# Matmul operands laid out anew: normed tiles 1280 bytes apart, weight blocks at one place modulo 256, small vectors moved into the gaps

## The chip, the cores and the metric

The kernel runs on one core of a Trainium2 chip. The metric is device time in microseconds of one execution; several runs are made and their median is compared. A profiled execution gives a trace of every instruction.

## The reference

Two transformer blocks run one after the other on 256 tokens of width 1024, in fp32. The first has a mixer of mLSTM heads and latent attention, a cross attention to 256 memory tokens, and a feed-forward layer of width 4096. The second prepends 16 meta tokens (272 columns from there on), has a SwiGLU layer of width 2816, a mixer of windowed attention and gated linear attention, and a second SwiGLU layer. Nearly all the work is products of a normed activation with a weight matrix:

```python
h = rmsnorm(x, norm_ffn_g[l])
x = x + jnp.square(jax.nn.relu(h @ w_ff1[l])) @ w_ff2[l]
...
h = h + 0.5 * swiglu(rmsnorm_2(h, ffn1_norm[l]), ffn1_w_gate[l], ffn1_w_up[l], ffn1_w_down[l])
u = rmsnorm_2(h, mix_norm[l])
(aq, ak, av, gq, gk, gv, gr, g_low, gate_a, gate_b) = jnp.split(u @ w_in[l], offsets, axis=-1)
```

## The kernel before

**Products.** Activations lie transposed in SBUF: a tile holds 128 of the 1024 features on the partitions and all tokens along the row. A product `h @ w` is made of 128x128 weight blocks (stationary, loaded by LDWEIGHTS) with 256 or 272 moving columns, in fp32r. To keep fp32 accuracy both sides are split into a high and a low part, so each block costs three matmuls, called a triple here: `wh` with the high tile (L1046), `wh` with the low tile (L1047), `wl` with the high tile (L1048). The pairs of tiles are `U`/`UL` (normed input, 8 tiles), `H`/`HLO` (hidden layer, up to 22 tiles) and `Y`/`YL` (heads' outputs). There are 2304 triples.

**Weights.** SP loads a unit of up to 1024 columns (two 128-row blocks of 512 columns, as a rule) into one of six `raw` buffers. ScalarE copies it to `wh` (L1385), VectorE subtracts to get `wl` (L1819). `wh` and `wl` have four halves each, `PITCH` elements apart; the low part of a unit lies in the other half of its pair (`low_half`). A unit serves four output tiles, so a unit of two blocks is eight triples. Then the next unit follows.

**Order.** A planner (`Plan`) writes one list of steps; PE, ScalarE and VectorE each run their part of it in that order. The second mixer is woven from many chains by a table of letters.

**Places in SBUF.** While TensorE streams one tile, it already loads the weights of the next matmul. Which places of SBUF these two reads touch at one time is set by three things:

- where tile k of `U` starts: with 256 columns the tiles are packed 1024 bytes apart (`part`). With 272 columns they are 1088 bytes apart, so their starts step by 64 bytes modulo 256;
- where a weight block starts in its half: `first_columns` shifts the blocks of the products named in `skew` by 16 elements (64 bytes) a step, until the block's place modulo 256 fits the number of its tile k;
- `wh` begins 64 bytes past the start of `U`, modulo 256 (the assertion on 320 modulo 1024 in `build`).

```python
skew = {"sw1": 0, "dn1": 0, "in2": g == 2, "gvr": g, "gab": 1}.get(name)
...
while skew is not None and (n * width // 16 + shift - k - skew) % 4:
    shift += 1
```

So the block for tile k lies 64 bytes past tile k modulo 256. That holds between the two matmuls of a pair as long as both belong to tiles of equal k modulo 4. `same_place` orders the blocks as k, k+4 for this reason: inside a unit the distance stays at 64. Where one unit ends and the next begins, the stream is tile k+4 and the weights loaded under it belong to tile k+1, so the distance is 128 there. The first group of `sw1` and the first groups of `in2` and `gvr` (`plain=1`) take k in plain order 0, 1, 2, ... and have other distances at nearly every block.

`sw1` and `dn1` are the first SwiGLU layer (272 columns), `in2`, `gvr` and `gab` the input products of the second mixer (272 columns, or 256 starting 64 bytes into the tile for the names in `NO_META`). `ff1a`, `ff1b`, `ff2a`, `ff2b` are the feed-forward layer of the first block, `sw2` and `dn2` the second SwiGLU layer; these have 256 columns.

**Small vectors.** Nine tiles of 6 to 32 elements a row (`gcol`, `emc`, `HST`, `DC`, `ST`, `ST2`, `nsink`, `QRS`, `QKG`) hold gate columns, softmax sums and the like. They lie between `vec` and `X`; `beyond` then pads so that `X` starts at 64 modulo 256.

Of the kernel before, what the change touches and what calls it, by code (L numbers as in the profile page):

```python
# [8 lines left out]
F32 = mybir.dt.float32  # L9
F32R = mybir.dt.float32r  # L10
# [4 lines left out]
P = 128  # L15
# [3 lines left out]
T2 = 272  # L19
# [1 line left out]
FF1 = 4096  # L21
FF2 = 2816
SLOT = 1024
PITCH = 1152
NRAW = 6
NHL = 4
SL = 4 * T2
# [225 lines left out]
def first_columns(name, g, i):  # L253


    ks, width = GEMM[name].units(g)[i], GEMM[name].width(g)
    skew = {"sw1": 0, "dn1": 0, "in2": g == 2, "gvr": g, "gab": 1}.get(name)
    at, shift = [], 0
    for n, k in enumerate(ks):
        while skew is not None and (n * width // 16 + shift - k - skew) % 4:  # L260
            shift += 1
        at.append(n * width + 16 * shift)
    return at
# [7 lines left out]
def split_blocks(parts, half, name, g, i):  # L271
    at, width = first_columns(name, g, i), GEMM[name].width(g)
    step = at[1] - at[0] if len(at) > 1 else width
    assert all(a == at[0] + n * step for n, a in enumerate(at)) and at[0] + len(at) * step <= PITCH
    return parts[:, half, at[0]:at[0] + len(at) * step].rearrange("p (k c) -> p k c", c=step)[:, :, 0:width]
# [618 lines left out]

def part(t, name, k, n):

    at = SL * (k // 4) + n * (k % 4) if name in ("Y", "YL") else n * k
    return t[name].rearrange("p k c -> p (k c)")[:, at:at + n]


def streamed(t, name, k, tag):

    if name in ("small", "uv", "o", "wq_x", "ff1a", "ff1b", "sw2"):
        return part(t, "U", k, T1), part(t, "UL", k, T1)
    if name in ("sw1", "in2", "gvr", "gab"):
        a = NMETA if name != "sw1" and tag[0] in NO_META else 0
        return t["U"][:, k, a:T2], t["UL"][:, k, a:T2]
    if name in ("memk", "memv", "ff2a", "ff2b", "out2", "dn2"):
        return part(t, "H", k, T1), part(t, "HLO", k, T1)
    if name == "dn1":  # L910
        return t["H"][:, k, :], t["HLO"][:, k, :]
    if name in ("uq", "ukv"):
        k = 2 if name == "ukv" else k
        return t["CQH"][:, k, :], t["CQL"][:, k, :]
    return part(t, "Y", k, T1), part(t, "YL", k, T1)
# [1512 lines left out]
def pool_program(e, t, plan, ev):  # L2428

    at, up = ev.at, ev.up  # L2430
    e.memset(t["GT"][:, :, :], 0.0).then_inc(*up("filled", "gates"))
    e.wait_ge(*at("filled", "gates"))
    e.memset(t["SY3"][64:128, 0:256], 0.0).then_inc(*up("filled", "squares"))
    e.wait_ge(*at("filled", "squares"))
    e.memset(t["S"][64:128, SL + 512:SL + 768], 0.0).then_inc(*up("filled", "key"))
    e.wait_ge(*at("filled", "key"))
    e.memset(t["QB"][0:64, :], 0.0).then_inc(*up("filled", "mlstm"))
    e.wait_ge(*at("filled", "mlstm"))
    e.wait_ge(*at("angle", 0))
    e.memset(t["S"][0:64, SL + 768:SL + 1024], 0.0).then_inc(*up("filled", "second_key"))  # L2440
    e.wait_ge(*at("gates", "max"))
    e.dma_start(t["d_max"], t["GT"][0:4, 3, :]).then_inc(*up("out_max", 0, by=16))
    e.wait_ge(*at("out_max", 0))
    e.dma_start(t["S"][:, 8 * SL:8 * SL + 1024].rearrange("p (h c) -> p h c", h=4),
                t["d_max"].partition_broadcast(128)).then_inc(*up("in_max", 0, by=16))
# [68 lines left out]
def build(nc, aps, out):  # L2514
    with ExitStack() as ctx:
        def sb(name, shape, dt=F32):
            return ctx.enter_context(nc.sbuf_tensor(name, shape, dt))

        def beyond(residue, modulus, name):
            if (residue - nc.sbuf_base) % modulus:  # L2520
                sb(name, [P, (residue - nc.sbuf_base) % modulus // 4])

        t = dict(aps)
        t["out"] = out
        t["cst"] = sb("cst", [P, NLAST])
        t["vec"] = sb("vec", [P, NVEC])
        t["gcol"] = sb("gcol", [P, 16])
        t["emc"] = sb("emc", [P, 8])
        t["HST"] = sb("HST", [P, 4, 8])
        t["DC"] = sb("DC", [P, 8])  # L2530
        t["ST"] = sb("ST", [P, 2, 6])
        t["ST2"] = sb("ST2", [P, 2, 16])
        t["nsink"] = sb("nsink", [P, 8])
        t["QRS"] = sb("QRS", [P, 8])
        t["QKG"] = sb("QKG", [P, 8])
        beyond(64, 256, "before_x")
        t["X"] = sb("X", [P, 8, T2])
        base = nc.sbuf_base
        for n in ("U", "UL"):
            t[n] = sb(n, [P, 8, T2], F32R)  # L2540

        for i, n in enumerate(("Y", "YL")):
            at = nc.sbuf_base
            t[n] = sb(n, [P, 8, T2], F32R)
            assert nc.sbuf_base == at + 8 * T2 * 4
            for j in range(2):
                t[f"SY{2 * j + i}"] = nc.alloc_sbuf_tensor_at(f"SY{2 * j + i}", [P, SL], F32, offset=at + j * SL * 4)
        t["S"] = sb("S", [P, 13 * SL])
        t["raw"] = sb("raw", [P, NRAW, SLOT])
        t["RS"] = sb("RS", [P, T2])  # L2550
        assert (nc.sbuf_base - base) % 1024 == 320
        t["wh"] = sb("wh", [P, NHL, PITCH], F32R)
        t["wl"] = sb("wl", [P, NHL, PITCH], F32R)
        t["G"] = sb("G", [P, 2, T2])
        t["RM"] = sb("RM", [P, T2])
        beyond((base + 512) % 1024, 1024, "before_h")
        t["H"] = sb("H", [P, 22, T2], F32R)
        top_h = nc.sbuf_base
        t["ACC"] = sb("ACC", [P, T2])
        beyond(base % 1024, 1024, "before_hlo")  # L2560
        t["HLO"] = sb("HLO", [P, 22, T2], F32R)
        top_hlo = nc.sbuf_base
        def over(top, *named):
            at = top - 14 * T2 * 4
            for name, shape, dt in named:
                at = (at + 31) // 32 * 32
                t[name] = nc.alloc_sbuf_tensor_at(name, shape, dt, offset=at)
                at += int(np.prod(shape[1:])) * 4
            assert at <= top, (named[0][0], at - top)

        over(top_h, ("HN", [P, 4, 256], F32))
        over(top_h, ("UR", [P, 4, 259], F32), ("CQH", [P, 3, 256], F32R), ("CQL", [P, 3, 256], F32R),
             ("SQB", [P, 1024], F32))
        over(top_h, ("AV", [P, 4, 192], F32), ("AVM", [P, 2, 128], F32), ("KDT", [P, 5, 256], F32), ("AT", [P, 2, T1], F32),
             ("ZZ", [P, 2 * T2], F32), ("AVT", [P, T2], F32))
        over(top_hlo, ("GT", [P, 6, 256], F32), ("PR", [P, 2, 512], F32), ("PT", [P, 2, 512], F32))
        over(top_hlo, ("GQ1", [P, 2 * T1], F32))
        t["glagw"] = nc.alloc_sbuf_tensor_at("glagw", [P, 256], F32, offset=nc.sbuf_base)
        t["wqk"] = sb("wqk", [P, 4, 128])
        at = nc.sbuf_base  # L2580
        t["PTM"] = sb("PTM", [P, 2, T1])
        t["GVm"] = sb("GVm", [P, 512])
        assert nc.sbuf_base == at + 1024 * 4
        t["QB"] = nc.alloc_sbuf_tensor_at("QB", [P, 1024], F32, offset=at)

        t["ps"] = [ctx.enter_context(nc.psum_tensor(f"ps{i}", [P, 512], F32)) for i in range(8)]

        plan, ev = Plan(), Events()
        for program in (pe_program, act_program, dve_program, pool_program, sp_program):
            program(Counting(), t, plan, ev)  # L2590
        ev.known, ev.count = ev.value, {}
        ev.sems = {n: ctx.enter_context(nc.semaphore(f"s_{n}")) for n in sorted({n for n, _ in ev.known})}
        block = ctx.enter_context(nc.Block())

        @block.sync
        def _(e):
            sp_program(e, t, plan, ev)

        @block.tensor
        def _(e):  # L2600
            pe_program(e, t, plan, ev)

        @block.scalar
        def _(e):
            act_program(e, t, plan, ev)

        @block.vector
        def _(e):
            dve_program(e, t, plan, ev)

        @block.gpsimd
        def _(e):
            pool_program(e, t, plan, ev)
# [64 lines left out]
```

## Time and profile before

| | us |
|---|---|
| Median of three runs | 912.51 |
| The three runs | 918.71, 912.08, 912.51 |
| The profiled execution | 918.25 |
| Its span, first to last instruction | 916.5 |
| PE busy in the span | 904.2 |
| PE weight load busy | 887.5 |
| VectorE busy | 642.7 |
| ScalarE busy | 525.4 |

The span is the part of the profiled execution that the trace shows; 1.8 us lie around it. PE busy is a sum over pipelined matmuls whose ends are modelled, so it tells only that TensorE hardly ever had nothing to do. How fast it went is read from the starts of its matmuls.

### The profile page before, as it was taken

What the parts mean: (1) busy time and instruction counts of PE and PEld (TensorE: products, weight loads), DVE (VectorE), ACT (ScalarE), POOL (GpSimd) and SP (SyncE); (2) the same over time, 40 slices, a digit from 0 to 9 for tenths busy, and PEclk for the clock granted to TensorE, in tenths of its full rate; (3) what the DMA queues carried; (4) which work ended last, traced back from release to release, by engine and by line L of the source; (5) the groups of instructions that cost most, each with busy time, mean ns of one, the idle gap of its engine ahead of it and who ended that gap; (6) DMA issues with size and microseconds to landing.
All of it is one profiled execution on the core that took longest, in us unless ns stands there. A gap on an engine that the chain in (4) does not pass through costs nothing.

```text
span 916.5 us, 18478 instructions
## 1 busy us (share of the span) xinstructions
PE 904.2 (99%) x7425; PEld 887.5 (97%) x7425; DVE 642.7 (70%) x1108; ACT 525.4 (57%) x869; POOL 4.7 (1%) x11
## 2 busy tenths in 40 slices
PE   9999999999999999999999999999999999999996
PEld 8988998999999999999999999999999999999996
DVE  6999888776446765676666547768769877767553
ACT  6897877666336655544444535445675665454452
POOL 1000000000000000000000000000000000000000
PEclk9999999999999999999999999999999999999998
DMA  9751444365765565555556465554415655665641
GB/s 312 248 171 72 139 139 161 93 206 187 234 185 179 175 192 183 171 176 171 179 185 202 149 184 161 161 171 130 162 50 203 186 185 187 198 201 198 208 138 46
DMA packets 110612, 157.63 MB, mean 172 GB/s; under 512 B 9916, under 2 KB 61248, under 8 KB 110400
## 3 DMA queue, kind: packets, MB, share of 16 engines
q1 hardware_dynamic: 109776, 155.19, 53.4%
q8 instruction: 60, 0.98, 0.4%
q10 hardware_dynamic: 576, 0.73, 0.2%
q0 software_dynamic: 176, 0.53, 0.1%
q14 instruction: 24, 0.20, 0.1%
HBM read 155.37 MB, written 1.05 MB: 171 GB/s over the span
## 4 chain that ended last, share of the span: by engine, by line
PE 95%; DVE 3%; ACT 1%; issue 1%; DVEq 0%; ACTq 0%
PE ps L1046 29%; PE ps L1048 29%; PE ps L1047 29%; PE ps L1093 1%; PE ps L1129 1%; PE ps L1060 1%; DVE wl L1819 1%; PE ps L1303 0%; PE ps L1323 0%; PE ps L1261 0%; PE ps L1283 0%; PE ps L1139 0%; ACT wh L1385 0%; DVE S L2070 0%; PE ps L1152 0%
## 5 line engine op out<-in xcount | busy, mean ns | idle before, releaser
L1819 DVE TENSOR_TENSOR wl<-raw,wh 128x1024 fp32r<-128x1024 f32 (+2 forms) x291 | 346.8, 1212 | 197.4 <-ACT wh L1385 196.8
L1385 ACT ACTIVATE wh<-raw 128x1024 fp32r<-128x1024 f32 (+2 forms) x291 | 298.1, 1046 | 193.4 <-PE ps L1048 193.0
L1046 PE MATMUL ps<-U,wh 128*128 128x256 f32 (+2 forms) x1392 | 398.3, 286 | 0.1
L1048 PE MATMUL ps<-U,wl 128*128 128x256 f32 (+2 forms) x1392 | 391.4, 281 | 0.0
L1047 PE MATMUL ps<-UL,wh 128*128 128x256 f32 (+2 forms) x1392 | 390.8, 281 | 0.0
L1046 PEld LDWEIGHTS ps<-U,wh 128*128 128x128 f32 (+1 forms) x1392 | 261.6, 188 | 3.1 <-issue 1.4
L1047 PEld LDWEIGHTS ps<-UL,wh 128*128 128x128 f32 (+1 forms) x1392 | 261.9, 188 | 1.7 <-issue 1.0
L1048 PEld LDWEIGHTS ps<-U,wl 128*128 128x128 f32 (+1 forms) x1392 | 262.3, 188 | 0.0
L1046 PE MATMUL ps<-H,wh 128*128 128x256 f32 (+1 forms) x736 | 208.7, 284 | 0.1
L1048 PE MATMUL ps<-H,wl 128*128 128x256 f32 (+1 forms) x736 | 206.6, 281 | 0.0
L1047 PE MATMUL ps<-HLO,wh 128*128 128x256 f32 (+1 forms) x736 | 206.4, 280 | 0.0
L1048 PEld LDWEIGHTS ps<-H,wl 128*128 128x128 f32 x736 | 139.4, 189 | 0.0
L1046 PEld LDWEIGHTS ps<-H,wh 128*128 128x128 f32 x736 | 138.3, 188 | 0.8 <-ACT QB L1655 0.5
L1047 PEld LDWEIGHTS ps<-HLO,wh 128*128 128x128 f32 x736 | 138.5, 188 | 0.3 <-issue 0.2
L1046 PE MATMUL ps<-Y,wh 128*128 128x256 f32 x160 | 45.4, 284 | 0.1
L1501 ACT ACTIVATE H<-S 128x272 fp32r<-128x272 f32 (+1 forms) x44 | 18.7, 425 | 45.7 <-DVE S L2010 45.7
L1047 PE MATMUL ps<-YL,wh 128*128 128x256 f32 x160 | 44.2, 276 | 0.0
L1048 PE MATMUL ps<-Y,wl 128*128 128x256 f32 x160 | 44.2, 276 | 0.0
L2059 DVE TENSOR_TENSOR HLO<-S,H 128x256 fp32r<-128x256 f32 (+1 forms) x84 | 35.8, 426 | 7.8 <-ACT H L1489 4.3
L1497 ACT ACTIVATE S<-S 128x272 f32<-128x272 f32 (+1 forms) x44 | 18.7, 425 | 33.4 <-DVE S L2005 33.4
L1473 ACT ACTIVATE U<-X,vec 128x256 fp32r<-128x256 f32 (+1 forms) x40 | 20.5, 512 | 23.2 <-DVE X L1983 14.9
L1046 PEld LDWEIGHTS ps<-Y,wh 128*128 128x128 f32 x160 | 30.0, 188 | 0.7 <-DVE wl L1819 0.4
(340 smaller groups left out, 788.5 us busy)
## 6 DMA issues: line engine op xcount, KB each, us to landing
raw<-w_ff SPq DMA_DIRECT2D x64, 512.0 KB, 4.4
raw<-ffn_w_gate SPq DMA_DIRECT2D x88, 256.0 KB, 3.7
raw<-ffn_w_up SPq DMA_DIRECT2D x88, 256.0 KB, 4.6
raw<-ffn_w_down SPq DMA_DIRECT2D x44, 512.0 KB, 4.6
raw<-w_in SPq DMA_DIRECT2D x40, 512.0 KB, 3.7
raw<-w_out SPq DMA_DIRECT2D x16, 512.0 KB, 3.9
raw<-wkv_x SPq DMA_DIRECT2D x8, 512.0 KB, 3.9
raw<-w_in SPq DMA_DIRECT2D x9, 256.0 KB, 3.1
```

Source lines behind the costliest of these rows:

```text
L1046: e.matmul(out, sh, xh, start=(i == 0 and n == 0), stop=False)
L1047: e.matmul(out, sh, xl, start=False, stop=False)
L1048: mm = e.matmul(out, sl, xh, start=False, stop=(over and n == nk - 1))
L1060: e.matmul(t["ps"][7][:, 0:256], t["RM"][:, 0:128], t["RM"][:, 0:256], start=True, stop=True)
L1093: e.matmul(pb, cst("halves" if tag in ("kr", "qr") else "ones"), sq[:, a:z], start=True, stop=True).then_inc(*up("norm_sum", (tag, i)))
L1129: mm = e.matmul(ps[:, o:o + n], q(h, a0, a0 + 128), k(h, 0, n), start=(i == 0), stop=(i == len(pairs) - 1))
L1385: e.activation(wh, raw, ACT.Copy).then_inc(*up("w_hi", v))
L1473: e.activation(part(t, "U", k, n), xs, ACT.Identity, scale=vec(GAIN[stage], k)).then_inc(*up("u_hi", (stage, k)))
L1497: e.activation(S(i, T2, T2 + T), S(i, 0, T), ACT.Silu).then_inc(*up("silu", (name, n)))
L1501: e.activation(part(t, "H", n, T), S(i, 2 * T2, 2 * T2 + T), ACT.Copy).then_inc(*up("h_hi", (name, n)))
L1819: lo = e.tensor_tensor(wl, raw, wh.bitcast(F32), ALU.subtract)
L2059: e.tensor_tensor(part(t, "HLO", n, T), full, part(t, "H", n, T).bitcast(F32), ALU.subtract).then_inc(*up("h_lo", (name, n)))
```

## The change

Tiles of `U` and `UL` with 272 columns are laid out 320 elements (1280 bytes, five times 256) apart, so all of them start at one place modulo 256; the packed 256-column form stays. `first_columns` no longer follows k, except for `dn1`, whose tiles (`H`) are still 1088 bytes apart. The halves of `wh` and `wl` are 1088 elements apart in place of 1152 (4352 bytes in place of 4608). The small vectors go into the 48-element gaps behind tiles 6 and 7 of `U` and `UL`. The order of instructions on every engine is the same as before. The units whose two blocks lay 528 columns apart lie contiguous now, so that their splits read `128x1024` and no longer `128x2x512`.

In the built program `vec` ends at byte 6948. Before, the small vectors followed it and `X` began at byte 7744, which is 64 modulo 256. Now the pad that `beyond` works out from 6948 is itself put at the next multiple of 32, 6976, and `X` begins at byte 7008, which is 96 modulo 256. Everything behind it keeps its place relative to `U` modulo 256, so `X`, `U`, `UL`, `Y`, `S`, `raw`, `H` and `HLO` begin at 32 modulo 64 where they began at 0 modulo 64, and so do `wh` and `wl`. Modulo 512 and 1024 some distances change too: `UL` lies 10240 bytes past `U` (0 modulo 1024) and not 8704 (512 modulo 1024), and neighbouring halves of `wh` are 256 apart modulo 512 and not 0.

```diff
@@ -21,7 +21,8 @@
-PITCH = 1152
+PITCH = 1088
+UP = 320
@@ first_columns
-        while skew is not None and (n * width // 16 + shift - k - skew) % 4:
+        place = k if name == "dn1" else 0
+        while skew is not None and (n * width // 16 + shift - place - skew) % 4:
             shift += 1
@@ part
-    at = SL * (k // 4) + n * (k % 4) if name in ("Y", "YL") else n * k
+    at = SL * (k // 4) + n * (k % 4) if name in ("Y", "YL") else (UP if name in ("U", "UL") and n == T2 else n) * k
@@ build
-        t["gcol"] = sb("gcol", [P, 16])
-        t["emc"] = sb("emc", [P, 8])
-        t["HST"] = sb("HST", [P, 4, 8])
-        t["DC"] = sb("DC", [P, 8])
-        t["ST"] = sb("ST", [P, 2, 6])
-        t["ST2"] = sb("ST2", [P, 2, 16])
-        t["nsink"] = sb("nsink", [P, 8])
-        t["QRS"] = sb("QRS", [P, 8])
-        t["QKG"] = sb("QKG", [P, 8])
         beyond(64, 256, "before_x")
         t["X"] = sb("X", [P, 8, T2])
         base = nc.sbuf_base
+        between = [(base + 4 * (8 * UP * i + UP * k + T2)) for i in range(2) for k in (6, 7)]
         for n in ("U", "UL"):
-            t[n] = sb(n, [P, 8, T2], F32R)
+            t[n] = sb(n, [P, 8, UP], F32R)
+        for at, named in zip(between, ((("gcol", [P, 16]), ("HST", [P, 4, 8])), (("emc", [P, 8]), ("DC", [P, 8]), ("ST2", [P, 2, 16])),
+                                       (("nsink", [P, 8]), ("QRS", [P, 8]), ("QKG", [P, 8])), (("ST", [P, 2, 6]),))):
+            for n, shape in named:
+                t[n] = nc.alloc_sbuf_tensor_at(n, shape, F32, offset=at)
+                at += int(np.prod(shape[1:])) * 4
```

Counted over the built program, pairs of neighbouring matmuls of these products whose distance (start of the next weights less start of the stream, modulo 256) is not 64:

| stage | columns | before | after |
|---|---|---|---|
| `sw1`, first group | 272 | 31 | 0 |
| `sw1`, other groups | 272 | 40 | 0 |
| `dn1` | 272 | 36 | 36 |
| second mixer, `U` | 272 | 39 | 4 |
| second mixer, `U` | 256 | 69 | 49 |
| `small` (blocks 1824 bytes apart) | 256 | 36 | 36 |
| `uq`, `ukv` | 256 | 48 | 48 |

The other products with 256 columns have 64 at every pair, before and after.

## Rows read from the trace of the kernel before

**Rows 1.** The page: busy us, share of the span, instructions; the chain by engine.

```profile
PE 904.2 (99%) x7425; PEld 887.5 (97%) x7425; DVE 642.7 (70%) x1108; ACT 525.4 (57%) x869; POOL 4.7 (1%) x11
...
PE 95%; DVE 3%; ACT 1%; issue 1%; DVEq 0%; ACTq 0%
```

**Rows 2.** Windows: busy us and instructions of each engine, TensorE's clock, DMA share.

```profile
184.00:355.00 171.00, 171.00 (x1454) 171.00 (x1454) 104.88 (x146) 91.19 (x135) 0.00 (x0) 1.00 0.62 197
368.14:474.99 106.85, 106.85 (x866) 106.85 (x865) 72.13 (x108) 50.98 (x73) 0.00 (x0) 1.00 0.58 178
553.00:700.00 147.00, 147.00 (x1191) 143.38 (x1191) 113.39 (x233) 84.13 (x154) 0.00 (x0) 1.00 0.47 144
735.00:906.00 171.00, 171.00 (x1511) 171.00 (x1511) 109.47 (x157) 84.86 (x117) 0.00 (x0) 1.00 0.55 176
```

**Rows 3.** Timeline, PE: triples before and behind a stop at 182.5.

```profile
181.44 0.28 PE L1046 MATMUL ps<-U,wh 128*128 128x256 f32 x1
...
181.78 0.28 PE L1046 MATMUL ps<-U,wh 128*128 128x256 f32 x1
...
182.46 0.59 PE L1076 MATMUL ps<-ACC,cst 128*128 128x256 f32 x2
183.12 0.39 PE L1046 MATMUL ps<-U,wh 128*128 128x256 f32 x1
...
184.29 0.28 PE L1046 MATMUL ps<-U,wh 128*128 128x256 f32 x1
...
184.64 0.28 PE L1046 MATMUL ps<-U,wh 128*128 128x256 f32 x1
```

**Rows 4.** Timeline, PE: first triples of sw1's first group.

```profile
355.66 0.29 PE L1046 MATMUL ps<-U,wh 128*128 128x272 f32 x1
...
357.92 0.28 PE L1046 MATMUL ps<-U,wh 128*128 128x272 f32 x1
```

**Rows 5.** Timeline, PE: sw1's first eight triples of the second group, and 36 units on.

```profile
368.14 0.29 PE L1046 MATMUL ps<-U,wh 128*128 128x272 f32 x1
...
368.51 0.28 PE L1046 MATMUL ps<-U,wh 128*128 128x272 f32 x1
...
371.10 0.29 PE L1046 MATMUL ps<-U,wh 128*128 128x272 f32 x1
...
437.15 0.28 PE L1046 MATMUL ps<-U,wh 128*128 128x272 f32 x1
437.27 0.29 PE L1047 MATMUL ps<-UL,wh 128*128 128x272 f32 x1
...
474.99 0.29 PE L1046 MATMUL ps<-U,wh 128*128 128x272 f32 x1
```

**Rows 6.** Timeline, PE: gab, the end of one unit (590.88) and the next.

```profile
589.86 0.28 PE L1046 MATMUL ps<-U,wh 128*128 128x256 f32 x1
...
590.20 0.28 PE L1046 MATMUL ps<-U,wh 128*128 128x256 f32 x1
...
590.88 0.28 PE L1046 MATMUL ps<-U,wh 128*128 128x256 f32 x1
...
591.23 0.28 PE L1046 MATMUL ps<-U,wh 128*128 128x256 f32 x1
...
591.58 0.28 PE L1046 MATMUL ps<-U,wh 128*128 128x256 f32 x1
```

**Rows 7.** Timeline, PE: small, the block at 32 modulo 64 and the next one.

```profile
12.76 0.28 PE L1046 MATMUL ps<-U,wh 128*128 128x256 f32 x1
...
13.12 0.28 PE L1046 MATMUL ps<-U,wh 128*128 128x256 f32 x1
...
13.47 0.28 PE L1046 MATMUL ps<-U,wh 128*128 128x256 f32 x1
```

**Rows 8.** Groups by line and shape: the weight splits on ScalarE and VectorE.

```profile
L1385 ACT ACTIVATE wh<-raw 128x1024 fp32r<-128x1024 f32 x281 | 290.0, 1054 | 187.7 <-PE ps L1048 187.6
...
L1819 DVE TENSOR_TENSOR wl<-raw,wh 128x1024 fp32r<-128x1024 f32 x281 | 337.6, 1222 | 195.0 <-ACT wh L1385 194.5
```

## Prediction

> **What bounds the kernel now.** I read the page first, for which engine has nothing to spare: TensorE, with 904.2 us busy of 916.5 and 95% of the chain that ended last [rows 1]. VectorE and ScalarE are at 70% and 57%. Busy time of pipelined matmuls tells no pace, so next I read windows and divide their length by the number of matmuls. In 184 to 355 us (`ff1a` to `ff2b`, 256 columns) 1454 matmuls take 171 us, 117.6 ns each; in 735 to 906 us (`sw2`, `dn2`, also 256 columns) 1511 take 171 us, 113.2 ns each [rows 2]. PE has no gap in either, the granted clock is 1.00 in both (2.4 GHz, the upper of its two levels), and DMA is busy 0.62 and 0.55 of the time. The same tiles at the same places, the same instructions, and two paces.
>
> So I looked in the timeline for where the pace changes. Up to 181.78 us a triple takes 0.34 us; then TensorE stops for the sum of squares (L1076) and for the next weights, and from 184.29 on a triple takes 0.35 us, and so until 355 [rows 3]. The reader is to see that nothing but the stop lies between. In `gab` the same switch happens without a stop: 0.34 us a triple before the end of a unit at 590.88, 0.35 us behind it [rows 6], and that unit's end is a place where the next weights lie 128 bytes, not 64, past the stream (modulo 256). So the reads of the stream and of the next weights seem to fall into one of two rhythms, 113.2 and 117.6 ns, and a stop or an ill-placed pair can change the rhythm. With 272 columns there is one: 865 matmuls in 106.85 us, 123.5 ns [rows 2].
>
> **What the change mends.** It acts on distances in the 272-column products on `U`, and on a few in the second mixer. Three terms, each with the count of pairs from the table in the change.
>
> First group of `sw1`, 32 triples: its first six take 357.92 - 355.66 = 2.26 us, 0.377 each [rows 4], where nearly every distance is off. A triple with none off takes 0.370 (368.51 - 368.14) [rows 5]. 32 x 0.007 = 0.2 us.
>
> Ends of units in the other ten groups of `sw1`, 40 pairs: 36 units are 288 triples, at 0.370 they would take 106.56 us; from 368.14 to 474.99 they took 106.85 [rows 5]. That is 0.29 us over 36 ends, 8 ns an end, and 0.3 us for 40. TensorE waits for nothing in this stretch, so the 0.3 us lie on the path.
>
> Second mixer: 35 pairs fewer off at 272 columns, 20 fewer at 256. At the same 8 ns, 55 x 0.008 = 0.4 us. The stage is part product, part small steps that wait on ScalarE and VectorE (PE loads weights 143.38 of its 147.00 us [rows 2]), so I take 0.3. `dn1` keeps all 36 of its bad pairs: 0.
>
> The sum is 0.2 + 0.3 + 0.3 = 0.8 us. A side effect in the same stage: an ill-placed end can no longer switch `gab` to the slow rhythm. From 553 to 700 us there are 650 matmuls with `wh` weights, which is two thirds of the products' matmuls; were all 975 to gain the 4.4 ns between the two paces, it would be 4 us at most, but half of them have 272 columns or run in the fast rhythm already, and a switch can also lead back to the fast one. I take 0 and keep 2 us for the lower end.
>
> **What it adds or moves without a gain.** The splits of skewed units become contiguous: 281 copies of 1054 ns on ScalarE and 281 subtractions of 1222 ns on VectorE [rows 8]; in stages where these engines are busy 51 and 72 us of 107 [rows 2] a difference of some ns in either is covered by TensorE. If that cover were gone, 281 x 0.01 us = 3 us is what 10 ns each would cost. The small vectors are read and written by the same instructions at another place. I take 0 for both. The order of instructions doesn't change, and no wait is added.
>
> The halves' new distance (256 modulo 512) and `UL`'s (0 modulo 1024) change distances modulo 512 and 1024 in every product. Before, both residues of 512 occur: from tile 0 to tile 4 of `sw1` the distance changes by 256 modulo 512 and not at all modulo 256, and the triple at 368.14 (tile 0) takes 0.37 us as does the mean of the eight up to 371.10, half of which are tile 4 [rows 5]. I take 0 for this.
>
> The one thing that no product of before shows is that streams and weights now start at 32 modulo 64. Only `small` has weights there, each second block, with the stream at 0 modulo 64 and so the distance off as well: such a triple takes 0.36 us (12.76 to 13.12), the one behind it 0.35 [rows 7], against 0.34 [rows 3]. That is the upper bound of the cost. The lower bound is a gain: if the shift brought every slow matmul to the fast pace. I take 0, since the distance of 64 stays and the absolute place has not mattered in steps of 64 bytes: in `gab` at 589.86 the stream starts at 128 modulo 256, at 181.44 at 64 modulo 256, and both give 0.34 [rows 3, 6]. The Trainium skill (SBUF — State Buffer, section on the port swizzle) says that SBUF has 16-byte lines and that an access pays when it crosses into a new one; a shift by 32 bytes keeps every start on such a line and would cost nothing. No row here shows the width of a line.
>
> **The sum.** The profiled execution took 918.25 us, 916.5 of span and 1.8 around it. Less 0.8 it is 917.4. That execution had 184 to 355 us in the slow rhythm; at the fast pace its 1454 matmuls take 1454 x 0.1132 = 164.6, which is 6.4 us less. Of the three runs two took 912.1 and 912.5 and one 918.7, just such a step apart, so I read the median as an execution with the fast rhythm there. 912.5 - 0.8 = **911.7 us**.
>
> **Rivals.**
>
> *The slow rhythm in the feed-forward layer* (chance 0.12). Which rhythm follows the stop at 182.5 us looks like a throw of the dice, two of four executions each way. If the median of after has the slow one: 911.7 + 6.4 = 918.1. That is still no change by the bound of 1%, 9 us, which is about what a measurement of this kernel can tell.
>
> *The misplacement by 32 bytes costs* (chance 0.15, slower). The change says that it puts things at one place, and it does, but at a place 32 bytes off. If a row at 32 modulo 64 makes each read touch one more line than before, both reads meet more often and the fast rhythm is lost in all products with 256 columns. There are about 5100 such matmuls (968 + 560 + 160 + 24 triples); I count some 900, in `small`, `memk` and the second mixer, that are slow already in the timeline. 4200 x 4.4 ns = 18.5 us, so 930 us; if all went to the 120 ns of `small` (0.36 / 3), 5100 x 6.8 ns = 35 us, 946 us. It decides slower as soon as a matmul loses over 2 ns. For it: the 0.36 in rows 7. Against: there the distance is off too, which alone would explain it.
>
> *The 272-column products find a faster rhythm* (chance 0.07 for some, 0.06 for enough). Ill-placed ends kick the rhythm every eight triples; without them it might settle lower. The shortest spacing in the rows is 0.12 us (437.15 to 437.27 [rows 5]). At 120 ns, 1248 matmuls on `U` would gain 3.5 ns, 4.4 us; with 2 us from the second mixer 911.7 - 6.4 = 905.3. With `dn1` and more of the 256-column products in it, 903 or less. Against: the eight triples from 368.14 on follow a whole group and have no bad pair among them, and stay at 0.370 [rows 5]. The Trainium skill (TensorE: Matmul & The Clock Gate, section on the back-to-back issue gap) gives N / 2.4 + 2.5 ns, 115.8 ns at 272 columns and 109.2 at 256, whatever the places are; the rows lie above both (123.5 and 113.2), so its rule is a floor that this kernel doesn't reach. If the change reached it on `U`, it would be 1248 x 7.7 ns = 9.6 us, by the page's figure.
>
> **How the numbers follow.** The forecast itself has 0.60. With the slow-rhythm case (0.12) and the smaller gain (0.07) that is 0.79 within 1% of 912.5; the misplacement 0.15 slower; 0.06 faster. For 8 in 10 the range must take in both rhythms and the 905 of the third rival: 904.5 to 922. The likeliest case's own range is 909.5 to 913.5 (2 us below for the second mixer).
>
> **What the profile of after would show.** Right: `sw1`'s units end without the 5 ns step and 36 units take 106.56 us; the first group's triples take 0.370; `gab` keeps one rhythm from stop to stop; `sw2` at 113.2 ns a matmul. Wrong: a pace in 735 to 906 us other than 113.2 (the 32 bytes matter), a pace in `sw1` under 123 (a new rhythm). What would make it wrong besides: a third rhythm that no execution before has shown, since the places modulo 64 are new to every product.

## The result and the profile after

The changed kernel takes 917.61 us in the median (15 runs, 917.10 to 924.49), the kernel before 912.11 us (15 runs beside it, 911.70 to 918.80). The ratio is 1.0063 [1.0046, 1.0080]: slower by 0.6%. The forecast was 911.7 us, a little faster than before. The measured time lies above the range of the likeliest case (909.5 to 913.5) and inside the wide range (904.5 to 922) that was to take in the rivals.

The times of either kernel come in two clusters, 6 to 7 us apart: 11 of the 15 before lie near 912.0 and 4 near 918.7, and 13 of the 15 after lie near 917.5 and 2 near 924.3. The whole pair of clusters has moved up by most of a step. Two runs told of below came at a lower mean granted clock than the 0.997 or more of the others, one of before (929.54 us, 0.948) and one of `e9_ones_at_128` (1119.27 us, 0.752), and are compared with nothing. The profiled execution of after took 917.99 us, 916.2 of it span. Its page, busy us and share of each engine, then the chain by engine:

```profile
PE 904.0 (99%) x7425; PEld 887.2 (97%) x7425; DVE 641.7 (70%) x1108; ACT 525.9 (57%) x869; POOL 4.7 (1%) x11
...
PE 91%; DVE 6%; ACT 1%; issue 1%; DVEq 0%; ACTq 0%
```

The busy times are those of [rows 1] within 1 us; an engine's busy time cannot show a pace. The chain has PE at 91% where it was 95%, but it is 91% in `e3_constants_too` and `e4_pitch_only` below as well, which have no loss, so that doesn't tell it either. The windows do. Those of after over the same stages, columns as in [rows 2] (the first ends at 348 us, since `ff2b` ends at 349):

```profile
184.00:348.00 164.00, 164.00 (x1450) 164.00 (x1449) 103.66 (x146) 91.37 (x135) 0.00 (x0) 1.00 0.64 204
349.24:456.00 106.76, 106.76 (x866) 106.68 (x865) 73.17 (x112) 54.78 (x79) 0.00 (x0) 1.00 0.58 177
553.00:700.00 147.00, 147.00 (x1199) 143.46 (x1198) 113.56 (x230) 84.46 (x150) 0.00 (x0) 1.00 0.47 147
735.00:906.00 171.00, 171.00 (x1454) 171.00 (x1454) 104.85 (x150) 80.69 (x110) 0.00 (x0) 1.00 0.51 164
```

The last row is the loss: 1454 matmuls in the 171 us of `sw2` and `dn2`, where [rows 2] has 1511. The first row is a gain of the same kind, 113.1 ns a matmul (164 / 1450) for 117.6 in [rows 2]; this one execution before happened to be in the slow rhythm there. The granted clock is 1.00 in all of them, and DMA is less busy in the slow stretch than before (0.51 for 0.55), so neither is the cause.

For a balance by stage I read the first matmul of each stage from the timeline. Of after, TensorE (start us, us, engine, line, operation, tiles): `ff1a`, `sw1`, `dn1`, `sw2`, the sum of squares at the end.

```profile
174.38 0.28 PE L1048 MATMUL ps<-U,wh 128*128 128x256 f32 x1
...
349.24 0.28 PE L1048 MATMUL ps<-U,wh 128*128 128x272 f32 x1
...
479.95 0.29 PE L1048 MATMUL ps<-H,wh 128*128 128x272 f32 x1
...
720.39 0.28 PE L1048 MATMUL ps<-U,wh 128*128 128x256 f32 x1
...
907.14 0.38 PE L1071 MATMUL ps<-ACC,cst 128*128 128x256 f32 x1
```

And of before (`sw1` begins with the first row of [rows 4]):

```profile
174.30 0.28 PE L1046 MATMUL ps<-U,wh 128*128 128x256 f32 x1
...
486.86 0.29 PE L1046 MATMUL ps<-H,wh 128*128 128x272 f32 x1
...
727.59 0.28 PE L1046 MATMUL ps<-U,wh 128*128 128x256 f32 x1
...
907.56 0.38 PE L1069 MATMUL ps<-ACC,cst 128*128 128x256 f32 x1
```

| stage | before, us | after, us | difference |
|---|---|---|---|
| `ff1a` to `ff2b` | 181.36 | 174.86 | -6.50 |
| `sw1` | 131.20 | 130.71 | -0.49 |
| `dn1` and second mixer | 240.73 | 240.44 | -0.29 |
| `sw2`, `dn2` | 179.97 | 186.75 | +6.78 |

The first row is the rhythm of `ff1a` to `ff2b` in these two executions. The two middle rows are the intended effect, 0.78 us. The last row is a side effect nearly nine times as large.

The place where `sw2` changes its rhythm can be seen. Timeline of TensorE in after, around the sum of squares of `sw2`, whose weights are the matrix of ones in `cst`:

```profile
725.83 0.28 PE L1048 MATMUL ps<-U,wh 128*128 128x256 f32 x1
...
726.17 0.28 PE L1048 MATMUL ps<-U,wh 128*128 128x256 f32 x1
...
726.51 0.59 PE L1078 MATMUL ps<-ACC,cst 128*128 128x256 f32 x2
726.75 0.47 PE L1048 MATMUL ps<-U,wh 128*128 128x256 f32 x1
...
727.29 0.28 PE L1048 MATMUL ps<-U,wh 128*128 128x256 f32 x1
...
727.65 0.28 PE L1048 MATMUL ps<-U,wh 128*128 128x256 f32 x1
...
728.00 0.28 PE L1048 MATMUL ps<-U,wh 128*128 128x256 f32 x1
```

The same place in before:

```profile
733.37 0.28 PE L1046 MATMUL ps<-U,wh 128*128 128x256 f32 x1
...
733.72 0.59 PE L1076 MATMUL ps<-ACC,cst 128*128 128x256 f32 x2
733.96 0.47 PE L1046 MATMUL ps<-U,wh 128*128 128x256 f32 x1
...
734.49 0.28 PE L1046 MATMUL ps<-U,wh 128*128 128x256 f32 x1
...
734.83 0.28 PE L1046 MATMUL ps<-U,wh 128*128 128x256 f32 x1
...
735.17 0.28 PE L1046 MATMUL ps<-U,wh 128*128 128x256 f32 x1
```

Both come to the sum at 0.34 us a triple. Before leaves it at 0.34, after at 0.35 to 0.36, and keeps that for the 510 triples that are left of `sw2` and `dn2`. No row shows a wait: the sum begins 0.34 us behind the start of the triple ahead (726.17 to 726.51), and the next triple begins 0.24 us behind the sum's start in both kernels. From the sum of `sw2` to the sum at the end it is 180.63 us in after (726.51 to 907.14) and was 173.84 us in before (733.72 to 907.56); 6.79 us over 510 triples is 13.3 ns a triple, 4.4 ns a matmul.

### The profile page after: what moved, and what is told of

Same layout as the page of the kernel before. It is cut to its first block, busy times and chain, and to the rows that moved or that the text cites. A ratio compares the mean times of both kernels' runs of the same rounds, so it can differ in the third digit from the quotient of the medians.

```text
span 916.2 us, 18478 instructions
## 1 busy us (share of the span) xinstructions
PE 904.0 (99%) x7425; PEld 887.2 (97%) x7425; DVE 641.7 (70%) x1108; ACT 525.9 (57%) x869; POOL 4.7 (1%) x11
## 4 chain that ended last, share of the span: by engine, by line
PE 91%; DVE 6%; ACT 1%; issue 1%; DVEq 0%; ACTq 0%
PE ps L1048 28%; PE ps L1050 28%; PE ps L1049 28%; DVE wl L1821 1%; PE ps L1131 1%; PE ps L1062 1%; ACT wh L1387 1%; PE ps L1095 1%; DVE S L2226 1%; PE ps L1305 0%; DVE S L2072 0%; PE ps L1325 0%; PE ps L1263 0%; DVE X L1985 0%; PE ps L1285 0%
```

## The experiments

Four things were different at that place, and each makes a theory: the start of `X` and all behind it, modulo 64 (theory B, the absolute place); distances modulo 512 and 1024 (theory C: `PITCH`, `UL`); the time of everything around it by some tenths (theory D, a matter of chance); and the distance between the fixed constants, which lie ahead of `X` and did not move, and all that moved with `X` (theory A). `ones` begins at byte 1152, 128 modulo 256; `U` began at 64 and begins at 96 modulo 256. So the weights of the sum lay 64 bytes past the stream ahead of them, and lie 32 bytes past it now. The sum's own moving tile, `ACC`, moved with `U` (from 192 to 224 modulo 256), so the distance of `ones` to it fell by the same 32 bytes. Below, "distance" is the one to the stream ahead; every kernel that changes it changes the one to `ACC` alike, and no experiment parts the two.

The table gives all ten kernels. "Low" and "high" count the runs in the clusters of that kernel; the last two columns are the matmuls in 160 us of TensorE's windows 185 to 345 and 735 to 895 us in the profiled execution (1414 is the fast rhythm, 1361 the slow one). A kernel's ratio to before mixes the clusters of both, so a share of clusters can move it: the kernel before was in its high one in 10 of the 31 runs beside `e1` to `e4`, in 7 of 29 beside `e5` to `e7`, and in 10 of 19 beside `e8` to `e10`. One more of the 31 is the run of 929.54 us.

| kernel | median, us | low / high cluster | ratio | ff | sw2 |
|---|---|---|---|---|---|
| `e1_x_at_64` | 917.27 | 5 / 7 | 1.0011 [0.9983, 1.0039] | 1361 | 1414 |
| `e2_before_plus_32` | 918.86 | 7 / 1 (918.4, 925.1) | 1.0067 [1.0039, 1.0095] | 1415 | 1361 |
| `e3_constants_too` | 914.65 | 6 / 6 | 1.0014 [0.9987, 1.0042] | 1414 | 1414 |
| `e4_pitch_only` | 912.12 | 8 / 4 | 1.0008 [0.9983, 1.0034] | 1415 | 1414 |
| `e5_sum_behind_stop` | 911.51 | 12 / 0 | 0.9982 [0.9963, 1.0001] | 1414 | 1414 |
| `e6_before_far_ones` | 918.95 | 8 / 4 (918.4, 924.9) | 1.0074 [1.0045, 1.0103] | 1415 | 1361 |
| `e7_after_near_ones` | 911.48 | 11 / 1 | 0.9979 [0.9957, 1.0001] | 1415 | 1414 |
| `e8_after_sum_behind_stop` | 924.53 | 0 / 4 | 1.0113 [1.0067, 1.0158] | 1361 | 1361 |
| `e9_ones_at_128` | 911.38 | 9 / 0, one run at 1119.27 | 0.9967 [0.9939, 0.9994] | 1414 | 1414 |
| `e10_ones_at_0` | 911.05 | 9 / 1 | 0.9949 [0.9922, 0.9975] | 1414 | 1414 |

### The shift by 32 bytes, undone and done alone

`e1_x_at_64`: after, with the pad worked out from where it is really put, so that `X` starts at byte 6976, 64 modulo 256.

```diff
         def beyond(residue, modulus, name):
-            if (residue - nc.sbuf_base) % modulus:
-                sb(name, [P, (residue - nc.sbuf_base) % modulus // 4])
+            start = (nc.sbuf_base + 31) // 32 * 32
+            if (residue - start) % modulus:
+                sb(name, [P, (residue - start) % modulus // 4])
```

> The changed kernel with everything from X on 32 bytes lower, at 64 modulo 256 as before (the pad is worked out from a rounded start); the constants stay at 128. Theory A (the constants didn't move with the rest: the weights of the sum of squares lie 32 bytes and not 64 past the stream ahead of it, and this turns the stop in sw2 to the slow rhythm every time): about 911.3 us, sw2 and dn2 at 113.3 ns a matmul, the 272-column stage at 370.0 ns a triple. Theory B (a start at 32 modulo 64 by itself): the same, 911.3. Theory C (distances modulo 512 and 1024, from PITCH and the place of UL): stays at 917.6 with the slow rhythm in sw2. Theory D (only the time at which the stop is reached has changed, by the mended pairs): stays at 917.6.

Measured: `sw2` is fast again. Its windows on TensorE (matmuls, clock, DMA share, GB/s):

```profile
185.00:345.00 160.00, 160.00 (x1361) 1.00 0.61 196
735.00:895.00 160.00, 160.00 (x1414) 1.00 0.59 188
```

The first window is the slow rhythm, and 7 of 12 runs were in the high cluster. So the median of 917.27 comes from the share of runs that are slow in the feed-forward layer; the low cluster lies near 911.2.

`e2_before_plus_32`: before, with `X` at 96 modulo 256 and nothing else changed.

```diff
-        beyond(64, 256, "before_x")
+        beyond(96, 256, "before_x")
```

> The kernel before with everything from X on 32 bytes further (96 modulo 256), the constants where they were, nothing else. Theories A and B: 6 us slower than before, about 918.5, with sw2 and dn2 in the slow rhythm (117.8 ns). Theories C and D: as before, 912.1, with the same share of executions near 918.7.

Measured: 918.86 us, 6.7 above before's low cluster, with 1361 matmuls in `sw2`'s window. The shift alone makes the loss, without any other part of the change; so D and C fall. A and B both stand.

### The constants shifted too

`e3_constants_too`: after, with 32 bytes ahead of `cst`. Now every tile is shifted alike and `X` still starts at 32 modulo 64.

```diff
         t["out"] = out
+        sb("before_cst", [P, 8])
         t["cst"] = sb("cst", [P, NLAST])
```

> The changed kernel with the constants and vec also 32 bytes further, so that their distance to streams and weights is as before modulo 256 and only the absolute start is at 32 modulo 64. Theory A: about 911.3, fast rhythm in sw2. Theory B: 917.6, slow rhythm in sw2. C and D: 917.6.

Measured:

```profile
185.00:345.00 160.00, 160.00 (x1414) 1.00 0.64 205
735.00:895.00 160.00, 160.00 (x1414) 1.00 0.55 175
```

Fast, with all starts at 32 modulo 64: B falls, and what counts is the distance between the constants and the rest. The low cluster is at 911.6, the other six runs at 917.8.

`e4_pitch_only`: before with the new distance of the halves.

```diff
-PITCH = 1152
+PITCH = 1088
```

> The kernel before with halves 1088 elements apart and not 1152, nothing else. Theory C: 6 us slower, about 918, slow rhythm in sw2. Theories A, B and D: as before, 912.1.

Measured: 912.12 us, both windows fast. From `dn1`'s first triple to the sum of `sw2` it takes 246.86 us, as before does, and from there to the sum at the end 173.84, as before does: no effect.

### The one matmul

`e6_before_far_ones`: before, with a copy of the ones at 32 bytes past the stream, read by this one sum only (`PTM` is a scratch tile free at the time). It adds one copy on VectorE and one wait on TensorE, for something long done.

```diff
+        ones = cst("ones")
+        if tag == "f2":
+            e.wait_ge(*at("zeroed", "ones_copied"))
+            ones = t["PTM"].rearrange("p a c -> p (a c)")[:, 40:168]
-        e.matmul(pb, cst("ones"), t["ACC"][:, 0:n], ...
+        e.matmul(pb, ones, t["ACC"][:, 0:n], ...
...
+        if (name, k) == ("out2", 0):
+            e.tensor_copy(t["PTM"].rearrange("p a c -> p (a c)")[:, 40:168], cst("ones")).then_inc(
+                *up("zeroed", "ones_copied"))
```

> The kernel before, with a copy of the 128x128 ones that is used for one matmul alone, the sum of squares in sw2 (tag f2), placed 32 bytes and not 64 past the stream ahead of it (modulo 256); one VectorE copy more. Theory A: this one matmul turns sw2 and dn2 to the slow rhythm: about 918.5 us, 117.8 ns a matmul from 735 to 906 us. Rival (it takes the 32 bytes at every use of the constants): 912.1 as before.

Measured: 918.95 us. Timeline of TensorE in this kernel at the sum:

```profile
726.60 0.28 PE L1046 MATMUL ps<-U,wh 128*128 128x256 f32 x1
...
726.94 0.28 PE L1046 MATMUL ps<-U,wh 128*128 128x256 f32 x1
...
727.29 0.59 PE L1080 MATMUL ps<-ACC,PTM 128*128 128x256 f32 x2
...
728.07 0.28 PE L1046 MATMUL ps<-U,wh 128*128 128x256 f32 x1
...
728.42 0.28 PE L1046 MATMUL ps<-U,wh 128*128 128x256 f32 x1
```

0.34 a triple ahead of it, 0.35 behind it, and 1361 in the window: the whole loss of 6.8 us from the place of the weights of one sum.

`e7_after_near_ones`: after with the same edit, columns 48 to 176, the copy 64 bytes past the stream.

> The changed kernel with a copy of the ones used for the sum in sw2 alone, placed 64 bytes past the stream (modulo 256); everything else stays 32 bytes off, the constants where they are. Theory A: 911.3 us in most executions, fast rhythm in sw2 and dn2, and since the sum in ff1a keeps the distance of 32, with which 20 of 23 executions so far kept the fast rhythm there, few near 917.8. Rival: 917.6.

Measured: 911.48 us, 11 of 12 runs in the low cluster. Its timeline at the sum:

```profile
726.23 0.28 PE L1048 MATMUL ps<-U,wh 128*128 128x256 f32 x1
...
726.57 0.59 PE L1082 MATMUL ps<-ACC,PTM 128*128 128x256 f32 x2
...
727.35 0.28 PE L1048 MATMUL ps<-U,wh 128*128 128x256 f32 x1
...
727.69 0.28 PE L1048 MATMUL ps<-U,wh 128*128 128x256 f32 x1
```

`e9_ones_at_128` and `e10_ones_at_0`: as `e7_after_near_ones`, with columns 0 to 128 (a distance of 128 bytes) and 32 to 160 (a distance of 0).

> The changed kernel with the copy of the ones for the sum in sw2 at 128 bytes past the stream. If only an offset inside 64 bytes is bad (the multiples of 64 are alike): 911.3, fast in sw2. If 64 is the one good distance, as for the weights of the products: 917.6 or more, slow in sw2.

> The same with the copy at distance 0. Only an offset inside 64 bytes is bad: 911.3. 64 is the one good distance: 917.6 or more.

Measured: 911.38 and 911.05 us, 1414 matmuls in `sw2` in both. So 64 is not the one good distance at the sum of `sw2`. Of the four tried (0, 32, 64, 128) only 32 is bad there. It is not the absolute place of the copy: at 96 modulo 256 it is bad in `e6_before_far_ones` and good in `e10_ones_at_0`.

In every kept trace TensorE came to this sum at the fast pace, 0.34 us a triple. So in `sw2` a distance of 0, 64 or 128 leaves the fast pace as it is, and 32 turns it to the slow one.

### The stop in the feed-forward layer

There the sum is followed by a wait for weights, in eight of the ten kept traces that have it at its old place. `e5_sum_behind_stop` is `e1_x_at_64` with the sum moved one output tile down, behind that wait.

```diff
+                    if (name, g, i, j) == ("ff1a", 0, 3, 0):
+                        self.run(self.rstd("ffn"))
...
         ff1a = self.gemm("ff1a")
-        self.run(ff1a, 12)
-        self.run(self.rstd("ffn"))
         self.run(ff1a)
```

> The kernel with X at 64 modulo 256 (the first of these experiments), and in ff1a the sum of squares issued one tile later: behind the first tile of the fourth unit, whose weights TensorE waits for, and no longer ahead of it. If the length of that wait throws the rhythm, and a sum that follows without a wait sets it to the fast one whatever it was (as in sw2), then all executions take about 911 us and none 917.5: better than both kernels. If the sum keeps the rhythm that it meets, the executions still split between 911 and 917.5.

Measured: 911.51 us, 12 of 12 runs between 910.97 and 912.23. The timeline of TensorE:

```profile
183.18 0.39 PE L1048 MATMUL ps<-U,wh 128*128 128x256 f32 x1 [0.51 <-DVE wl L1821]
...
183.63 0.28 PE L1048 MATMUL ps<-U,wh 128*128 128x256 f32 x1
...
183.99 0.59 PE L1078 MATMUL ps<-ACC,cst 128*128 128x256 f32 x2
...
184.77 0.28 PE L1048 MATMUL ps<-U,wh 128*128 128x256 f32 x1
...
185.11 0.28 PE L1048 MATMUL ps<-U,wh 128*128 128x256 f32 x1
```

The triple behind the wait takes 0.36 us (183.63 to 183.99), the slow rhythm; behind the sum it is 0.34. Here a sum at a distance of 64 with no wait behind it brings the fast rhythm back.

`e8_after_sum_behind_stop`: the same move in after, where the distance is 32.

> The changed kernel as it is (constants 32 bytes past the stream, modulo 256), with the sum of squares in ff1a issued behind the first tile of the fourth unit. If a sum at the distance of 32 sets the slow rhythm whatever went before, as it does in sw2, then ff1a to ff2b and sw2, dn2 are slow in all executions: about 924 us. If the distance matters in sw2 alone: 917.6, and no 924.

Measured: 924.53 us, all four runs within 0.6, and both windows slow:

```profile
185.00:345.00 160.00, 160.00 (x1361) 1.00 0.62 196
735.00:895.00 160.00, 160.00 (x1361) 1.00 0.58 187
```

It differs from `e5_sum_behind_stop` by 32 bytes in the place of `X`, and by 13.0 us: two stretches, of about 487 and 510 triples, at 13.3 ns a triple, are 13.3 us. In its trace the last triple between the stop and the sum of `ff1a` takes 0.36 us, so the rhythm was slow already, and there the sum kept it and didn't make it.

A distance of 32 does not always lead to the slow rhythm. In the traces of `e7_after_near_ones` and `e9_ones_at_128`, whose sum in `ff1a` still reads the constants at 32, TensorE came to it at the slow pace with no stop before or behind it. Timeline of TensorE in `e7_after_near_ones`:

```profile
182.23 0.28 PE L1048 MATMUL ps<-U,wh 128*128 128x256 f32 x1
...
182.58 0.28 PE L1048 MATMUL ps<-U,wh 128*128 128x256 f32 x1
...
182.94 0.59 PE L1082 MATMUL ps<-ACC,cst 128*128 128x256 f32 x2
183.18 0.47 PE L1048 MATMUL ps<-U,wh 128*128 128x256 f32 x1
...
183.72 0.28 PE L1048 MATMUL ps<-U,wh 128*128 128x256 f32 x1
...
184.06 0.28 PE L1048 MATMUL ps<-U,wh 128*128 128x256 f32 x1
```

Ahead of the sum a triple takes 0.35 to 0.36 us, behind it 0.34. So a sum at 32 turned the fast rhythm to the slow one in `sw2` (four traces), the slow one to the fast one here (two traces), and left the slow one in `e8_after_sum_behind_stop` (one trace). The rhythm behind it depends on more than this distance.

## Why the prediction was wrong

**The size of the intended gain was right.** Of the sum of 0.8 us, the two terms of `sw1` (0.2 and 0.3) are 0.49 us in the balance, the second mixer (0.3) and `dn1` (0) together 0.29. All twelve traces agree: `sw1` takes 131.20 to 131.24 us in the four kernels with the old layout and 130.70 to 130.71 in the eight with the new one, and from `dn1`'s first triple to the sum of `sw2` it is 246.86 to 246.95 and 246.56 to 246.63 us. The starts in `sw1` say the same. Timeline of TensorE in after, the last triple ahead of a sum and the triples behind it up to the end of that stretch:

```profile
355.53 0.28 PE L1048 MATMUL ps<-U,wh 128*128 128x272 f32 x1
...
356.74 0.28 PE L1048 MATMUL ps<-U,wh 128*128 128x272 f32 x1
...
474.77 0.29 PE L1048 MATMUL ps<-U,wh 128*128 128x272 f32 x1
```

From the first start at 349.24 to 355.53 are 17 triples, 0.370 us each, where [rows 4] had 0.377. From 356.74 to 474.77 are 319 triples in 118.03 us, 0.3700 each, where [rows 5] had 106.85 / 288 = 0.3710. (The prediction's list of signs calls the step at an end of a unit 5 ns; its own sum has it as 8 ns, and 8 is what [rows 5] give.) Whether the medians show the 0.8 is less sure: `e7_after_near_ones`, which is after with the sum mended, lies at 911.4 in its low cluster and before at 912.0, in the same direction, and the interval of its ratio ends at 1.0001.

**The side effect in `gab`** (0 taken, 2 us kept) was about 0. From 580 to its next stop at 597 us it does keep one rhythm, as expected, and that is the slow one. Timeline of TensorE in after, two rows of that stretch:

```profile
583.19 0.28 PE L1048 MATMUL ps<-U,wh 128*128 128x256 f32 x1
...
593.79 0.28 PE L1048 MATMUL ps<-U,wh 128*128 128x256 f32 x1
```

They are 30 triples apart: 10.60 / 30 = 0.353 us each, where [rows 6] has both rhythms. Well-placed pairs alone did not lead back to the fast rhythm.

**Splits, small vectors, distances modulo 512 and 1024** (0 each): nothing in the balance is left for the splits and vectors, and `e4_pitch_only` shows 0 for the halves' distance. `UL`'s distance was in `e1_x_at_64`, with a low cluster at 911.2: no loss.

**The step that failed** is the last of the costs: "I take 0, since the distance of 64 stays and the absolute place has not mattered in steps of 64 bytes". The second half holds even in steps of 32 bytes (`e3_constants_too`). The first half holds only between operands that moved together. The ones of the sum of squares are weights too, they lie ahead of `X`, and their distance went from 64 to 32. The term put at 0 measured 6.8 us (`e2_before_plus_32`, and `e6_before_far_ones` for this one matmul). The reading of [rows 3] had prepared the mistake. It counted the sum, the row at 182.46, as a part of the stop, and concluded "nothing but the stop lies between". With the stop taken as what throws the rhythm, `sw2`, where nothing stops, looked safe at 113.2 ns. With the missing term the forecast would have been 911.7 + 6.8 = 918.5; 917.6 was measured, and the 0.9 between them was not traced. The runs showed that what turns the rhythm in `sw2` is the sum.

**The rivals.** *The misplacement by 32 bytes costs* had the right 32 bytes and the right sign but the wrong mechanism and price: no matmul loses by itself at 32 modulo 64, so it was not 930 to 946 us. One ill-placed sum puts the 510 triples behind it in the slow rhythm. *The slow rhythm in the feed-forward layer* gave 918.1 and is the nearest number, but by luck, since it was not that rhythm: of after's 15 runs only two were slow there, and they lie at 924.3. *The 272-column products find a faster rhythm* did not come true; the triples stay at 0.370. "A pace in 735 to 906 us other than 113.2 (the 32 bytes matter)" was the sign named beforehand, and it is what the profile shows.

On the pages: by the 16-byte lines of the Trainium skill (SBUF — State Buffer, section on the port swizzle) a shift by 32 bytes keeps starts on a line and costs nothing. For the absolute place `e3_constants_too` agrees; for the distance between a stream and the next weights `e6_before_far_ones` measured 6.8 us, which that rule doesn't foresee. The formula that the third rival took from the Trainium skill (TensorE: Matmul & The Clock Gate, section on the back-to-back issue gap) is given there for an isolated matmul, and the section says that for a stream of weight loads and matmuls it under-counts at few columns and over-counts at many, so it isn't the floor that the prediction made of it. This case's paces lie above it, 113.3 ns for 109.2 at 256 columns and 123.3 for 115.8 at 272.

**What stays open.** Where the sum meets a stop, in `ff1a`, the throw is not fair. With the sum's weights at a distance of 32 there, the slow rhythm came in 5 of 54 runs (after, `e2_before_plus_32`, `e7_after_near_ones`, `e9_ones_at_128`, `e10_ones_at_0`); at 64 in 21 of 48 (`e1_x_at_64`, `e3_constants_too`, `e4_pitch_only`, `e6_before_far_ones`) and in 31 of the 94 of the kernel before, the reverse of what it does in `sw2`. Why was not settled. The length of the stop doesn't show it: in the eight traces that have it the next triple begins 0.66 to 0.67 us behind the sum's start, whether the rhythm behind is slow (before, `e1_x_at_64`) or fast (the other six). Why a sum at 32 turned the slow rhythm to the fast one in two traces and kept it in a third is open too, and so is which of its two neighbours counts, the stream ahead or `ACC`. For 0 and 128 only the fast rhythm was ever ahead. What the two rhythms are inside the chip, and whether distances of 16 or of 96 bytes are bad too, wasn't tried.

## What to carry to other kernels

When buffers are moved to keep a distance between two operands, list every operand that TensorE takes as weights, the fixed constants included (the ones of the sum of squares here), and work out all distances from the addresses of the built program, not from a pad's argument. Where a pace lasts over hundreds of identical instructions and differs between executions, look at the last instruction ahead of it that differs from the rest (here the sum of squares), not at the stretch itself, and compare clusters of times, not medians alone. Such an instruction can be used: with `X` at 64 modulo 256 and the sum put behind the wait, it took the chance out of the feed-forward layer (`e5_sum_behind_stop`, 911.51 us, no run above 912.3, against a kernel before that was in its high cluster in 31 of its 94 runs).

## What the runs showed of the hardware

- A stream of fp32r triples with 256 columns runs at one of two paces, 113.3 or 117.8 ns a matmul (340.0 and 353.3 ns a triple), and kept it over 510 triples, 174 or 181 us, where no other instruction, stop or ill-placed pair came (before and after, `sw2` and `dn2`). At 272 columns with well-placed pairs only one pace was seen, 370 ns a triple (after, `sw1`).
- One sum of squares (two passes over 256 columns) can turn the pace of all that follows. Met at the fast pace in `sw2`, with its weights 0, 64 or 128 bytes past the preceding stream modulo 256 it left the fast pace, at 32 it led to the slow one (`e6_before_far_ones`, `e7_after_near_ones`, `e9_ones_at_128`, `e10_ones_at_0`). That is 6.8 us of 912 from the place of one 128x128 matrix.
- Met at the slow pace in `ff1a` with no stop behind it, the sum led to the fast one at 64 (`e5_sum_behind_stop`, 0.36 to 0.34 us a triple) and at 32 in two traces (`e7_after_near_ones`, `e9_ones_at_128`), and left the slow one at 32 in a third (`e8_after_sum_behind_stop`).
- Start addresses at 32 modulo 64 cost nothing by themselves (`e3_constants_too`, 1414 matmuls in 160 us as at 0 modulo 64).
